# A two-layer decoder trunk: the roles of weights and activations on TensorE exchanged, the norms made token-major

## The reference, cut to what matters

```
c_act = silu(c)
mod = c_act @ ada_w[l] + ada_b[l]          # (1024) @ (1024, 9216): shift, scale, gate of three sub-layers
modulate(t, i) = rms_norm(t, norm_g[l, i]) * (1 + scale(i)) + shift(i)
x = x + 0.5 * gate(0) * swiglu(modulate(x, 0))         # d_ff = 2816: wg, wu (1024, 2816), wd (2816, 1024)
z = modulate(x, 1) @ w_in[l]                           # (1024, 6400): q, k, v, u, gates
y_attn = merge of three dilated window attentions, 4 heads of 64 each, softmax over them, @ attn_wo
y_conv = silu(layer_norm(depthwise_conv31(a * sigmoid(g)))) @ conv_wo
y = sigmoid(g_attn) * y_attn + sigmoid(g_conv) * y_conv
x = x + gate(1) * (y @ w_out[l])
x = x + 0.5 * gate(2) * swiglu(modulate(x, 2))
```

## Time and profile before

| | us |
|---|---|
| median of three runs | 1379.12 |
| span of the profiled execution, first to last instruction | 1379.0 |
| start and first feed-forward stage, to the first matmul of mixing | 256.2 |
| mixing, layer 0 | 258.0 |
| second feed-forward stage | 200.05 |
| third | 203.25 |
| mixing, layer 1 | 260.9 |
| fourth feed-forward stage and the end | 200.6 |

### The profile page before, as it was taken

How to read it: one execution, slowest core, us unless ns; L and a number is a source line. 1 busy time by engine, 2 the same in 40 slices (tenths; PEclk the granted TensorE clock), 3 DMA queues, 4 the chain that set the end, 5 groups by cost and what they waited for, 6 DMA issues and landing times.

```text
span 1379.0 us, 24125 instructions
## 1 busy us (share of the span) xinstructions
PE 1297.4 (94%) x9992; PEld 1254.2 (91%) x9992; DVE 1035.6 (75%) x1220; ACT 573.8 (42%) x619; POOL 37.4 (3%) x50
## 2 busy tenths in 40 slices
PE   2699999899999899999989999989999989999997
PEld 1699999899888889999989999989988879899997
DVE  6998886798989766876577876678998976644444
ACT  2333334532335644443353333352323574533333
POOL 0010000000000010000000000000000000000000
PEclk8799999999999999999999999999999999999999
DMA  9989995335434366987827988623452525455550
GB/s 375 339 291 371 373 351 174 105 108 188 132 122 160 115 229 208 371 303 277 319 93 269 370 280 280 202 91 124 152 184 68 180 89 189 145 185 183 182 182 31
DMA packets 182600, 289.28 MB, mean 210 GB/s; under 512 B 4240, under 2 KB 163088, under 8 KB 176272
## 3 DMA queue, kind: packets, MB, share of 16 engines
q1 hardware_dynamic: 176784, 225.58, 48.9%
q0 software_dynamic: 5760, 62.92, 12.3%
HBM read 287.43 MB, written 1.05 MB: 209 GB/s over the span
## 4 chain that ended last, share of the span: by engine, by line
PE 78%; DVE 12%; ACT 4%; DMA 4%; issue 1%; SPq 0%; DVEq 0%; ACTq 0%
PE ps L386 23%; PE ps L387 23%; PE ps L388 23%; PE ps L422 5%; DVE work L1132 4%; DVE w_lo L938 3%; DMA raw<-in_w_in 2%; ACT w_hi L747 2%; PE ps L439 1%; DVE rstd L955 1%; DMA arena<-in_ada_w 1%; PE ps L450 1%; DVE arena L1277 1%; DMA raw<-in_ffn_wg 1%; PE ps L433 1%
## 5 line engine op out<-in xcount | busy, mean ns | idle before, releaser
L386 PE MATMUL ps<-hA_hi,w_hi 128*128 128x256 f32 x2016 | 581.5, 288 | 24.6 <-DVE hA_lo L974 20.4
L938 DVE TENSOR_TENSOR w_lo<-raw,w_hi 128x2048 fp32r<-128x2048 f32 x184 | 421.6, 2291 | 206.0 <-ACT w_hi L753 140.9
L387 PE MATMUL ps<-hA_lo,w_hi 128*128 128x256 f32 x2016 | 575.7, 286 | 0.0
L388 PE MATMUL ps<-hA_hi,w_lo 128*128 128x256 f32 x2016 | 575.6, 286 | 0.0
L386 PEld LDWEIGHTS ps<-hA_hi,w_hi 128*128 128x128 f32 x2016 | 392.4, 195 | 31.7 <-issue 29.4
L387 PEld LDWEIGHTS ps<-hA_lo,w_hi 128*128 128x128 f32 x2016 | 392.5, 195 | 0.2
L388 PEld LDWEIGHTS ps<-hA_hi,w_lo 128*128 128x128 f32 x2016 | 392.3, 195 | 0.0
L753 ACT CAST w_hi<-raw 128x2048 fp32r<-128x2048 f32 x108 | 206.4, 1911 | 245.6 <-PE ps L388 245.6
L1132 DVE SCALAR_TENSOR_TENSOR work<-conv_in,par,work 128x256 f32<-128x256 f32 x480 | 194.4, 480 | 0.0
L747 ACT CAST w_hi<-raw 128x2048 fp32r<-128x2048 f32 x76 | 144.4, 1904 | 112.8 <-PE ps L388 51.3
L386 PE MATMUL ps<-mid_hi,w_hi 128*128 128x256 f32 x672 | 187.2, 279 | 0.0
(11 more groups left out here) (102 smaller groups left out, 1108.0 us busy)
## 6 DMA issues: line engine op xcount, KB each, us to landing
arena<-in_ada_w POOLq DMA_DIRECT2D x40, 1536.0 KB, 6.7
raw<-in_w_in SPq DMA_DIRECT2D x50, 1024.0 KB, 5.6
raw<-in_ffn_wg SPq DMA_DIRECT2D x44, 1024.0 KB, 7.5
raw<-in_ffn_wu SPq DMA_DIRECT2D x44, 1024.0 KB, 6.0
raw<-in_ffn_wd SPq DMA_DIRECT2D x44, 1024.0 KB, 4.9
arena<-in_ada_w SPq DMA_DIRECT2D x12, 1024.0 KB, 10.3
raw<-in_conv_wo SPq DMA_DIRECT2D x8, 1024.0 KB, 6.7
raw<-in_w_out SPq DMA_DIRECT2D x8, 1024.0 KB, 5.0
```

The costliest lines, as they stand in the source:

```text
L386: nc.tensor.matmul(out_ap, stat[0], mov[0], start=start, stop=False, **kw)
L387: nc.tensor.matmul(out_ap, stat[0], mov[1], start=False, stop=False, **kw)
L388: return nc.tensor.matmul(out_ap, stat[1], mov[0], start=False, stop=stop, **kw)
L938: return nc.vector.tensor_tensor(dst, whole, hi_part.bitcast(F32), ALU.subtract)
```

## The change

Nearly every line is rewritten. What it does:

- The stationary operand is now a 128 x 128 piece of the activations and the weights move, 512 columns at a time: a panel is 4 blocks of k by 512 columns for k-panels (two panels, k 0 to 3 and 4 to 7, make 512 output columns), times two token tiles. The result has tokens on the partitions. Panels are laid out by the host (`weights[p]`, 8 KB for each partition), and `ada_w` in chunks of 128 x 1024 (0.5 MB).
- `RAW = 6` slots for loads, of which `w_lo` overwrites `raw` in place, and `HI = 5` slots of `w_hi`. Ten panels of each mixing stage are whole.
- Norms work on x as [tokens, 1024]: a square with an accumulated sum on ScalarE, a root, a reciprocal of 128 x 1, a scaling on VectorE, then eight 128 x 128 transposes a token tile on TensorE (`norm_turn`), and modulation in the evacuation. The last panels of a stage are ordered so that token tile 0 is finished, added and normed ahead of tile 1, and the next stage starts with tile 0.
- The modulation is 144 row sums: `ada_w` chunks (output channel on the partitions) times a broadcast `c`, with `accum_out`. There are no transposes or reductions. Gates go through DRAM to be broadcast.
- The silu product, GLU output, q and k, convolution output, its normed form and y are transposed on TensorE, where each was used as it came before. The rotary turn is three multiplications and an addition from PSUM on VectorE.
- The convolution's 248 taps a layer are laid out by new counts, and the rest is issued after the attention output has been gated.

The diff, cut to its core:

```diff
+PW = 2048
+M_U, M_QK, M_V0, M_V1, M_G, M_AO, M_G3, M_CO, M_WO = 0, 8, 14, 16, 17, 23, 24, 26, 30
+RAW = 6
+HI = 5
+WHOLE = (5, 7, 9, 11, 13, 15, 18, 20, 22, 25)
+QUOTA = (0, 0, 0, 2, 5, 9, 4, 9, 4, 9, 1, 9, 1, 9, 1, 7)
+HEAD_QUOTA = (6, 6, 6)
+ADA_AT = (16, 64, 104, 144)
+ADA_RING = 7
...
+            def three(out_ap, stat, mov, start, stop):
+                nc.tensor.matmul(out_ap, stat[0], mov[0], start=start, stop=False)
+                nc.tensor.matmul(out_ap, stat[0], mov[1], start=False, stop=False)
+                return nc.tensor.matmul(out_ap, stat[1], mov[0], start=False, stop=stop)
...
+            def k_half(p, h, tt, b, out_ap, last=None):
+                t = slice(tt * P, (tt + 1) * P)
+                for i in range(4):
+                    k, c = 4 * b + i, slice(512 * i, 512 * i + 512)
+                    if is_whole(p):
+                        mm = nc.tensor.matmul(out_ap, hF[:, k, t], raw[:, p % RAW, c], start=(k == 0), stop=(k == KC - 1))
+                    else:
+                        hi, lo = parts(p)
+                        mm = three(out_ap, (h[0][:, k, t], h[1][:, k, t]), (hi[:, c], lo[:, c]), k == 0, k == KC - 1)
...
+                for j in range(2, NJ - 1):
+                    both(g[j][0], hA, 0, gu(j))
+                    turn(f, j - 1, (0, 1))
+                    both(g[j][1], hA, 1, gu(j))
+                    down(f, j - 1, 0)
+                    down(f, j - 1, 1)
...
+                k_half(pb, hA, 0, 1, ps[:, gu(j), :], half_done)
+                down(f, j - 1, 0)
+                turn(f, j, (0,))
+                k_half(pa, hA, 1, 0, ps[:, gu(j) + 1, :])
+                down(f, j, 0, last=first_done)
+                k_half(pb, hA, 1, 1, ps[:, gu(j) + 1, :])
+                down(f, j - 1, 1, (0,))
+                turn(f, j, (1,))
+                down(f, j - 1, 1, (1,))
+                if n + 1 < NORMS - 1:
+                    norm_turn(n + 1, 0)
+                down(f, j, 1)
...
+                ready(base + M_AO)
+                pe.wait_ge(o_lo_done, 2 * l + 2)
+                for tt in range(TT):
+                    t = slice(tt * P, (tt + 1) * P)
+                    two_chunks(base + M_AO, (o_hi[:, :, t], o_lo[:, :, t]), tt, (0, 1), True, True, ao_done)
+                pe.wait_ge(raw_gate_done, 3 * (l + 1))
+                for pr in range(4):
+                    pe.wait_ge(conv_step, KC * TAPS * l + (pr + 1) * 2 * TAPS)
...
+                pe.wait_ge(ya_done, 4 * (l + 1))
+                group(M_G3, 0, 2)
+                group(M_G3 + 1, 1, 2)
+                for hf in range(2):
+                    pe.wait_ge(ln_xn_done, 4 * l + 2 * hf + 2)
...
+            def ada(q):
+                nc.vector.scalar_tensor_tensor(out=product[:, q % 2, :], in0=ada_raw[:, q % ADA_RING, :], scalar=1.0, in1=c_bc[:],
+                                               op0=ALU.mult, op1=ALU.mult,
+                                               accum_out=mods[:, g, n:n + 1]).then_inc(ada_step, 1)
...
+                conv(QUOTA[3])
+                for i in range(4, 16):
+                    if i in (6, 8):
+                        gated(i // 2 - 1)
+                    if i in (10, 12, 14):
+                        rotate((i - 10) // 2)
+                    lo(base + i + 3)
+                    conv(QUOTA[i])
+                for h in range(HPG):
+                    masked(h)
+                    lo(base + 19 + 2 * h)
+                    conv(HEAD_QUOTA[0])
+                    row_scales(h)
+                    conv(HEAD_QUOTA[1])
+                    lo(base + 20 + 2 * h)
+                    conv(HEAD_QUOTA[2])
+                    if h == 2:
+                        head_out(0)
+                head_out(1)
+                dve.wait_ge(sig_gate_done, 2 * l + 1)
+                for tt in range(TT):
+                    if tt == 0:
+                        dve.wait_ge(ao_done, l + 1)
...
+                        nc.vector.tensor_tensor(y[:, tt, c], acc(half, tt), gates[:, tt, c], ALU.mult).then_inc(ya_done, 1)
+                conv(taps_total)
+                for hf in range(2):
+                    dve.wait_ge(cT_done, 4 * l + 2 * hf + 2)
...
```

More of the change, by code:

```diff
@@ L56, in splits @@
     l, i = divmod(p, LAYER_PANELS)
[L57 to L74, removed]
-    with ExitStack() as ctx:
+    return p - l * len(WHOLE) - sum(w < i - FFN_PANELS for w in WHOLE)
@@ L141, in decoder_program, with cols @@
         T0 = S0
-        def pair(bank):
+        def cols(bank):
             return ps[:, bank, :].rearrange("p (c t) -> p c t", t=T)
[L146 to L156, removed]
@@ L189, in decoder_program @@
[L189 to L205, removed]
@@ new lines, in v1 @@
+                def v1(tt):
+                    p = base + M_V1
+                    hi, lo = parts(p)
+                    t = slice(tt * P, (tt + 1) * P)
+                    for k in range(KC):
+                        c = slice(k * 256, k * 256 + 256)
+                        mm = three(ps[:, 4 + tt, 0:256], (hA_hi[:, k, t], hA_lo[:, k, t]), (hi[:, c], lo[:, c]),
+                                   k == 0, k == KC - 1)
+                    if tt == 1:
+                        mm.then_inc(panel_done, 1)
@@ L689, in conv_sums @@
-                def conv_sums(first, last):
-                    pe.wait_ge(conv_step, KC * TAPS * l + last * TAPS)
-                    for k in range(first, last):
-                        mm = nc.tensor.matmul(ps[:, B_STAT, 0:T], ones[:], work[:, k, :], start=(k == 0),
-                                              stop=(k == KC - 1))
-                    return mm
-                conv_sums(0, 6)
-                conv_sums(6, KC).then_inc(ln_sum, 1)
-                split_ready(base + M_AO)
@@ new lines, in mix @@
+                pe.wait_ge(qk_done, 2 * (NG * l + 2))
+                group(M_V0, 0, 6)
+                qk_turn(2)
+                group(M_V0 + 1, 1, 6)
+                scores(0)
+                ready(base + M_V1)
+                v1(0)
+                v1(1)
+                pe.wait_ge(v_done, 2 * l + 1)
+                group(M_G, 0, 6, (0,))
+                p_turn(0)
+                group(M_G, 0, 6, (1,))
+                pv(0)
+                scores(1)
+                group(M_G + 1, 1, 6)
@@ new lines, in mix @@
+                hi(base + 9)
+                gated(2)
+                hi(base + 10)
+                conv_input(2)
+                hi(base + 11)
+                gate_store(n)
+                gated(3)
+                hi(base + 12)
+                conv_input(3)
+                hi(base + 13)
+                gate_load(n)
+                preload(ACT.Exp)
+                for g in range(NG):
+                    hi(base + 14 + 2 * g)
+                    qk_copy(g)
+                    hi(base + 15 + 2 * g)
@@ new lines, in mix @@
+                hi(base + 33)
+                hi(end)
+                hi(end + 1)
+                norm_square(n + 1, 0)
+                norm_std(n + 1, 0)
+                norm_full(n + 1, 0)
+                norm_hi(n + 1, 0, 0)
+                norm_hi(n + 1, 0, 1)
+                hi(end + 2)
+            act_e.wait_ge(c_in, 16)
+            nc.scalar.activation(c_bc[:], c_bc[:], ACT.Silu).then_inc(c_ready, 1)
+            act_e.wait_ge(setup_done, 2)
+            preload(ACT.Sqrt)
+            for tt in range(TT):
+                norm_square(0, tt)
+                norm_std(0, tt)
@@ L1105, in ada_dmas @@
[L1105 to L1111 removed]
+                s = splits(p)
+                dve.wait_ge(hi_done, s + 1)
+                minus(w_lo[:, p % RAW, :], raw[:, p % RAW, :], w_hi[:, s % HI, :]).then_inc(lo_done, 1)
@@ new lines, in finish_gate, with ada_units @@
+            def finish_gate(g, q):
+                o = C_LAYER * (g // 3) + C_ADAB + (g % 3) * 3 * KC + 2 * KC
+                dve.wait_ge(ada_step, q + 1)
+                nc.vector.tensor_tensor(gcol[:, g, :], mods[:, g, 2 * KC:3 * KC], par[:, o:o + KC],
+                                        ALU.add).then_inc(gcol_done, 1)
+            def ada_units(first, last):
+                for q in range(first, last):
+                    ada(q)
+                    g, w, k = ADA[q]
+                    if k == KC - 1 and w == 1 and g > 0:
+                        finish_norm(g, None, q)
+                    elif k == KC - 1 and w == 2:
+                        finish_gate(g, q)
@@ L1113, in mix, with conv @@
             def mix(l):
-                base = mix_base(l)
-                norm(3 * l + 1)
-                lo(base + 2)
+                base, n, end = mix_base(l), 3 * l + 1, mix_base(l) + MIX_PANELS
                 taps_total = KC * TAPS
-                def conv(first, last):
-                    for s in range(first, min(last, taps_total)):
+                done = 0
+                def conv(count):
+                    nonlocal done
+                    for s in range(done, min(done + count, taps_total)):
```

1839 lines of the change are left out of this document (922 added, 917 removed).

## The result

The changed kernel takes 1405.5 us (median of four runs, 1404.2 to 1406.3) against 1379.0 us before (four runs on the same chip): a ratio of 1.019, with a 95% interval of 1.018 to 1.0205. It is slower by 26.5 us (a little under 2%), 48 us above the forecast and outside its range. The profiled execution took 1404.2 us and has a span of 1402.4 us; stages are read from it. The time is thus 1.8 us above the span of the same execution, here and, within 0.2 us, in every later run of the whole kernel; the forecast let one number stand for both.

A forecast was written before the change was run, and what follows sets the result against it. The prediction took the count and pace of TensorE's instructions to bound the kernel. Its stages summed as 226 + 289 + 183 + 183 + 289 + 187.5 = 1357.5 us, 21.5 us (1.6%) faster, with a range from 1325 to 1392.

The forecast's parts named there:

- I take 216, a panel of 5.18 us: Split panels: each fp32r matmul of 512 columns takes 216 ns, as the f32 record does; all panels 1072 us, 84 less.
- the bounds (213.3 to 240): Fp32r matmul of 512 columns: 213.3 ns with no loss, 2 x 120 = 240 ns with no gain.
- Rival 1: Split panels: the loss of 13 ns stays at each matmul, 226 ns instead of 216; 1400 us, chance 0.13.
- At `mid`'s loss of 7 ns it would be 1375: Aside on split panels: with the 7 ns that mid loses at each matmul, the whole kernel would take 1375 us.
- The tail of taps: Mixing: 106 of 248 taps come after the attention output's gating, so TensorE idles 43.5 us a layer.
- the lower clock: Mixing, after the gap for taps: two M_G3 panels run partly at a lower clock, 3 us added a layer.
- Start: Start of the kernel: after norms and row sums TensorE begins at about 34 us with panels 0 and 1.
- Hand-overs: Between feed-forward stages: TensorE waits 2.7 us, 1.3 for the modulated tile and 1.5 where tile 1 meets lo(base + 3).
- Row sums with read-out and feeding: First feed-forward stage: feeding 3 to 9 us, read-out up to 9, mostly hidden; 2 us added for both.
- Rival 3: First three feed-forward stages: row sums with read-out and DMA at 368 GB/s are not hidden; 1377 us, chance 0.12.
- Rival 2: Mixing: the taps don't stand alone, the tail is covered and 2 x 43.5 us are saved; 1270 us, chance 0.04.
- Rival 4: Matmuls of 512 columns: loads and matmuls overlap beyond one column a period, 131 ns each; 1180 us, chance 0.01.

The follow-up runs named there:

- e1: Decoder left out of the changed kernel: 38 groups of 24 matmuls on TensorE alone, with other start addresses, types or columns; 262.8 us in all, one run.
- e6: Changed kernel with the same 248 taps dealt out earlier (13 between head_out(1) and the gating) and head_out(0) right behind masked(2); 1331.6 us, 0.966 of before.
- e4: Changed kernel with the weight buffers moved by 64 B, the rest where it stood modulo 128; 1419.1 us, 1.028 of before.
- e3: Changed kernel with the working region rounded up to 128 B, so that mid, hB and o start at 0; 1404.6 us, 1.018 of before.

## Why the prediction was wrong

- **The step that failed: "I take 216, a panel of 5.18 us".** The matmul of 512 columns takes 227.1 ns with `hA` and 234.2 with `mid`, `attn_wo` and `w_out`. 124 x 24 x 11.1 ns + 54 x 24 x 18.2 ns = 56.6 us, so the panels come to 1129 us and not 1072: the change saves 27 us of them, not 84. The panels of `mid` and the like did not gain at all, 5.45 us before and 24 x 234.2 ns = 5.62 now. I took the f32 record as nearest; it has another type, and in e1 f32 loses 2.5 ns over its periods in each record (215.8, 429.2) where fp32r loses 13 or more, so its small loss says nothing of fp32r. The row of the same type, 120 ns at 256 columns, gave the right answer to within 1 ns: 106.7 + 13.3, and 213.3 + 13.3 = 226.6. Both values stood in the bounds (213.3 to 240); the choice between them was wrong, and with it the sign, since by the forecast's own count slower begins at 221 ns.
- **Rival 1 was what happened**, at its price: 1400 forecast, 1402.4 measured (span). Its chance of 0.13 was too low: it rested on a row of the same type, the forecast on one of another. That its time comes so near is luck in part: it lacks some 14 us of the step (43 priced, 56.6 by the steps), and hand-overs that came 10.5 us cheaper and the early start make up for most. Its aside, "At `mid`'s loss of 7 ns it would be 1375", has the wrong sign: at 512 columns `mid` loses 21 ns and `hA` 14.
- **The tail of taps: right.** 43.5 us a layer forecast, 41.8 + 1.4 measured, 106 taps at 0.394 us. Of the 3 us for the lower clock 1.8 came there; the second stretch at the lower level, before `conv_wo`, is in no term of the sum (2.9 us in layer 0). e6 shows the price of the tail by removing most of it: 73.9 us of the 2 x 43.5.
- **Start: right, but forecast 2 us too late.** TensorE's first panel matmul is at 31.8 us (34 forecast).
- **Hand-overs: forecast 3.5 us too dear each.** I had 2.7 + 1.3 + 1.5. On the timeline of after, between the second and third feed-forward stage (idle time before it in brackets):

```profile
713.61 1.09 PE L371 MATMUL ps<-ident_sb,xn_h 128*128 128x128 f32 x8 [1.31 <-DVE xn_h L1038]
718.17 0.47 PE L320 MATMUL ps<-w_hi,hA_hi 128*128 128x512 f32 x1 [0.67 <-DVE hA_lo L959]
```

  2.0 us, and nothing at tile 1. Three such places are 10.5 us, most of the difference between the 56.6 us of the step and the 44.9 us by which the span is over the forecast.
- **Row sums with read-out and feeding: hidden, as forecast.** The two groups of instructions of after:

```profile
L974 DVE SCALAR_TENSOR_TENSOR product<-ada_raw,c_bc 128x1024 f32<-128x1024 f32 x144 | 171.0, 1220 | 2.3 <-DMA ada_raw<-in_ada_w 2.2
...
L974 DVE DVE_READ_ACCUMULATOR product<-ada_raw,c_bc 128x1 f32 x144 | 11.9, 83 | 0.0
```

  A sum takes 1.22 us, where 1.28 was assumed, and its read-out is an instruction of its own of 83 ns. In 570 to 709 us TensorE waits for nothing at a DMA share of 0.87. Rival 3 is out.
- **Rival 2** (the tail is covered) is not this kernel, but it is what e6 makes of it. **Rival 4** (131 ns) is out by every step measured.

## What to carry to other kernels

Price a matmul by a row of its own type, and split its step into columns over the clock and a loss: with `hA` the loss of fp32r stayed near 13 ns at twice the length, so one matmul of 512 columns took 227 ns where two of 256 took 240; with `mid` it rose from 7 to 21, 234 ns where two took 227. When one engine issues a background job in shares written out by hand, count how much is still due at the point where the next engine wants it all; here moving those shares was worth 73.9 us, and the whole gain in panels 27. Separate a type's gain from a layout's by applying it to both kernels before crediting either.

## What the runs showed of the hardware

- At 2.4 GHz an fp32r matmul loses 13 to 16 ns over its columns from 256 to 512 columns, with TensorE alone and all starts on 128 B, and takes 110 ns at 192 and at 128 columns; BF16 loses 2.5 ns and takes 55.8 at 128.
- At 1.2 GHz fp32r has no such loss: 426.7 ns at 512 columns (kernel after, 470.70 to 475.82), 213.3 at 256 (kernel before, 256.74 to 261.22).
- The start addresses of an fp32r matmul's operands move its step by up to 8 ns (226.5 to 234.3 in e1; 227.1 to 233.3 for `hA` in e4, 14 us of the kernel). The same move of 64 B that made `hA` slower at 512 columns made it faster at 256 (119.8 to 115.7). No rule by address modulo 128 B fits e1, e3 and e4 together; that is open.
- An f32 matmul of 512 columns is two records of 429 ns, of 256 columns two of 216: four clock periods a column in all.
- After 43 us with TensorE nearly idle (granted clock 0.56 in that window) four transposes and six matmuls ran at the lower level, at a cost of 1.8 us; after a wait of 4.83 us 14 matmuls did, at 2.9 us.
